# Hybrid SSD/MLA/GLA encoder on one core: the state-space heads' work taken up one head earlier, with other buffers and banks

## What is computed

```
proj = h @ w_in                                  # z, xbc, dt, q_a, kv_a
xbc  = silu(dwconv(xbc) + b);  xs, b_in, c_in = split(xbc)
dt   = softplus(dt_raw + dt_bias);  a = -exp(a_log)
# per head (16 of them), per direction (2), chunks of 128 tokens:
diff   = acum[l] - acum[s]
scores = (c @ b^T) * exp(where(causal, diff, -inf)) * dt[s]
y      = scores @ xs + (carried state) + xs * d_skip
y      = rmsnorm(y * silu(z))                    # two groups of 8 heads
o_mla  = attention(q_a, kv_a)                    # 8 latent attention heads
out    = concat(y, o_mla) @ w_out
```

## Time and profile before

| | us |
|---|---|
| median of 3 runs | 1443.49 (1442.85 to 1446.71) |
| the profiled execution | 1441.75 |
| its span, first to last instruction | 1439.6 |
| PE busy in it | 1379.3 (96%) |
| DVE busy | 822.8 (57%) |
| ACT busy | 646.5 (45%) |
| POOL busy | 639.9 (44%) |

### The profile page before, as it was taken

The page is one execution under the profiler, slowest core; times in us unless marked ns, Lnnn a source line. Parts: engine busy times, 40 slices in busy tenths (PEclk is TensorE's granted clock), DMA queues, the critical chain, the costliest instruction groups (busy, mean ns, idle before and its releaser), DMA issues.

```text
span 1439.6 us, 16672 instructions
## 1 busy us (share of the span) xinstructions
PE 1379.3 (96%) x6690; PEld 1138.9 (79%) x6690; DVE 822.8 (57%) x981; ACT 646.5 (45%) x985; POOL 639.9 (44%) x291
## 2 busy tenths in 40 slices
PE   6999988989999999999999999987999999999997
PEld 6778656767888888888888877875798888888886
DVE  5657597662027998887001654355168998884003
ACT  4544685554245544344323475434454544343221
POOL 2345495024533554545544243422714645445550
PEclk9999999999999999999999999998999999999998
DMA  5222100112322323323332312201213232323331
GB/s 188 86 92 88 37 1 19 33 45 88 99 77 90 101 93 98 95 95 94 93 95 86 114 59 88 88 30 44 73 45 131 89 102 89 102 85 94 96 92 59
DMA packets 36766, 117.89 MB, mean 82 GB/s; under 512 B 3857, under 2 KB 8337, under 8 KB 36689
## 3 DMA queue, kind: packets, MB, share of 16 engines
q1 hardware_dynamic: 35888, 114.63, 25.1%
q10 hardware_dynamic: 800, 2.20, 0.5%
HBM read 114.58 MB, written 2.10 MB: 81 GB/s over the span
## 4 chain that ended last, share of the span: by engine, by line
PE 76%; DVE 6%; ACT 3%; POOL 2%; issue 1%; DVEq 0%; ACTq 0%; POOLq 0%
PE bank L315 23%; PE bank L316 23%; PE bank L317 23%; PE bank L1169 1%; PE bank L1301 1%; POOL ebuf L987 1%; PE bank L1302 1%; POOL xdt L973 1%; PE bank L1777 1%; PE bank L1324 1%; DVE xres L562 1%; PE bank L405 1%; ACT prob L1373 1%; DVE m_ffn L555 0%; PE bank L1505 0%
## 5 line engine op out<-in xcount | busy, mean ns | idle before, releaser
L298 POOL TENSOR_TENSOR wlo<-raw,whi 128x1024 fp32r<-128x1024 f32 (+2 forms) x216 | 530.7, 2471 | 697.3 <-ACT whi L292 697.3
L315 PE MATMUL bank<-xw_hi,whi 128*128 128x512 f32 (+1 forms) x1360 | 516.6, 380 | 16.3 <-DVE xw_lo L581 11.7
L317 PE MATMUL bank<-xw_hi,wlo 128*128 128x512 f32 (+1 forms) x1360 | 505.8, 372 | 0.0
L316 PE MATMUL bank<-xw_lo,whi 128*128 128x512 f32 (+1 forms) x1360 | 505.8, 372 | 0.0
L292 ACT ACTIVATE whi<-raw 128x1024 fp32r<-128x1024 f32 (+2 forms) x217 | 220.6, 1023 | 216.5 <-DMA raw<-in_fout 111.8
L315 PEld LDWEIGHTS bank<-xw_hi,whi 128*128 128x128 f32 x1360 | 259.9, 191 | 67.8 <-issue 16.4
L316 PEld LDWEIGHTS bank<-xw_lo,whi 128*128 128x128 f32 x1360 | 259.8, 191 | 47.3 <-issue 3.6
L317 PEld LDWEIGHTS bank<-xw_hi,wlo 128*128 128x128 f32 x1360 | 259.5, 191 | 45.1
L534 DVE RECIPROCAL small<-small 128x2 f32<-128x2 f32 (+1 forms) x12 | 2.0, 170 | 352.7 <-ACT small L471 337.4
L638 DVE SCALAR_TENSOR_TENSOR cbuf<-ubuf,par,cbuf 128x510 f32<-128x510 f32 x100 | 170.8, 1708 | 3.5
L315 PE MATMUL bank<-g_hi,whi 128*128 128x512 f32 (+1 forms) x396 | 146.0, 369 | 0.1
(11 more groups left out here) (251 smaller groups left out, 1435.2 us busy)
## 6 DMA issues: line engine op xcount, KB each, us to landing
raw<-in_fin SPq DMA_DIRECT2D x88, 512.0 KB, 3.5
raw<-in_fout SPq DMA_DIRECT2D x32, 448.0 KB, 3.2
raw<-in_gin SPq DMA_DIRECT2D x25, 512.0 KB, 3.6
raw<-in_hin SPq DMA_DIRECT2D x24, 512.0 KB, 3.6
raw<-in_hout SPq DMA_DIRECT2D x16, 512.0 KB, 3.5
raw<-in_fout SPq DMA_DIRECT2D x16, 512.0 KB, 3.5
raw<-in_gout SPq DMA_DIRECT2D x8, 512.0 KB, 3.6
xres<-in_x SPq DMA_DIRECT2D x8, 256.0 KB, 7.5
```

The lines of the kernel that those rows point to most:

```text
L298: engine.tensor_tensor(wlo[s][:, 0:n], raw[s][:, 0:n], whi[s][:, 0:n].bitcast(F32), ALU.subtract).then_inc(w_lo, 1)
L315: first = nc.tensor.matmul(out_ap, wh, ah, start=start, stop=False)
L316: nc.tensor.matmul(out_ap, wh, al, start=False, stop=False)
L317: return first, nc.tensor.matmul(out_ap, wl, ah, start=False, stop=stop)
```

## The change

The diff moves work to earlier places and gives other buffers. It adds and removes no arithmetic.

- **Banks.** Block 20 goes to bank 0, blocks 21 and 23 to bank 7, block 22 to bank 6. The wait for `cb_set` moves from block 21 to block 22.
- **Buffers.** `ebuf3` lies in the region of the projection's input, `ebuf2` behind `xtok[0]` instead of over it, so the wait for xdt 0 to 3 is gone. Head 3's first step on ACT waits instead for the last block of the projection. The rotary key gets buffers of its own (`kr_part`).
- **Head 2 into the projection.** PE spreads head 2 after block 22, ACT takes its exponentials before silu of block 22, DVE its difference and mask before it scales block 23, POOL its mask after the weight part of block 25.
- **One head ahead.** DVE's turn n now holds the difference of head n+3 and the mask of head n+2. `gated` stays where it was. ACT's squares come one odd turn later.
- **POOL.** The 768 column weight part and both parts of xdt 4 stand ahead of mask 3. The additions of squares stand in even turns from 8 on.
- **End.** The sum of squares on PE stands after y(14) instead of y(13), and the two products of the rotary key ahead of gated(7).

The core of the diff:

```diff
-            return bank[(4, 5)[j] if j < 2 else 7 - j % 2 if j >= 20 else (0, 1, 3)[(j - 2) % 3]]
+            return bank[(4, 5)[j] if j < 2 else 6 + j % 2 if j >= 21 else (0, 1, 3)[(j - 2) % 3]]
...
             def gate(j):
                 his(act, base + j)
+                if j == 22:
+                    act_exps(act, 2)
...
             for n in range(HEADS):
-                if n + 2 < HEADS:
-                    dve_least(dve, n + 2)
-                if n >= 2:
-                    dve_mask(dve, n)
+                if n + 3 < HEADS:
+                    dve_least(dve, n + 3)
+                if 1 <= n < HEADS - 2:
+                    dve_mask(dve, n + 2)
                 if n % 2 and n >= 3:
                     gated((n - 3) // 2)
             dve_mla_low(dve)
+            dve_mla_rotated(dve)
             gated(KD - 1)
...
-            if n == 2:
-                act.wait_ge(sem("xdt_pool"), 4)
-                act.wait_ge(sem("xdt_dve"), 4)
+            if n == 3:
+                act.wait_ge(mm, BASE["hin"] + 24)
...
+            los(pool, BASE["mla"] - 1)
             pool.wait_ge(sem("xtok_dve"), NBLK)
-            for n in range(2, HEADS):
+            pool_xdt(pool, 4, 0)
+            pool_xdt(pool, 4, 1)
+            for n in range(3, HEADS):
                 pool_mask(pool, n)
-                if n < 10:
-                    pool_xdt(pool, 4 + (n - 2) // 2, n % 2)
-                if n % 2 and n >= 7:
-                    add_square((n - 7) // 2)
-                if n == HEADS // 2:
-                    los(pool, BASE["mla"] - 1)
+                if n < 9:
+                    pool_xdt(pool, 5 + (n - 3) // 2, (n - 3) % 2)
+                if n % 2 == 0 and n >= 8:
+                    add_square((n - 8) // 2)
```

More of the change, by code:

```diff
@@ L140, in build_program @@
             xdt = [None, None] + [sb(f"xdt{p}", 2 * NBLK * P, F32, s) for p in range(2, PAIRS * 2)]
+            ebuf3 = sb("ebuf3", 3 * T, F32, s)
+        with ExitStack() as s:
+            kr_part = [sb(f"kr_part{i}", T, F32, s) for i in range(2)]
         with ExitStack() as s:
@@ L160, in build_program @@
                 xbc = sb("xbc", 12 * T, F32, q)
-                with ExitStack() as q2:
-                    xtok = [sb("xtok0", NBLK * T, F32, q2), xtok_late]
-                ebuf_late = [sb(f"ebuf{i}", 3 * T, F32, q) for i in (2, 3)]
+                xtok = [sb("xtok0", NBLK * T, F32, q), xtok_late]
+                ebuf2 = sb("ebuf2", 3 * T, F32, q)
                 sqbuf = [sb(f"sqbuf{i}", T, F32, q) for i in range(2)]
@@ L183, in build_program @@
             sb("zbuf_mq", 12 * T, F32, s)
-            ebuf = [sb(f"ebuf{i}", 3 * T, F32, s) for i in range(2)] + ebuf_late
+            ebuf = [sb(f"ebuf{i}", 3 * T, F32, s) for i in range(2)] + [ebuf2, ebuf3]
             cbm = sb("cbm", 4 * 3 * SEQ, F32, s)
@@ L1102, in square @@
                                      ACT.Square).then_inc(sem("ssd_sq"), 1)
-            for n in range(2, HEADS):
+            for n in range(3, HEADS):
                 act_exps(act, n)
-                if n % 2 and n >= 5:
-                    square((n - 5) // 2)
+                if n % 2 and n >= 7:
+                    square((n - 7) // 2)
+            square(KD - 3)
             act_mla_prep(act)
@@ L1242, in pe_mla_prep, with dve_mla_rotated @@
             nc.tensor.matmul(bank[3][:], con("selrot"), ck(mq, 0), start=True, stop=True).then_inc(sem("mla_kr"), 1)
+        def dve_mla_rotated(dve):
+            dve.wait_ge(sem("rope_in"), 16)
+            dve.wait_ge(sem("mla_kr"), 1)
+            for i in range(2):
+                nc.vector.tensor_tensor(kr_part[i][:], bank[2 + i][:], cosin[:, i * T:(i + 1) * T],
+                                        ALU.mult).then_inc(sem("mla_kd"), 1)
         def dve_mla_prep(dve):
-            dve.wait_ge(sem("mla_kr"), 1)
-            nc.vector.tensor_tensor(ubuf[0][:], bank[2][:], cosin[:, 0:T], ALU.mult).then_inc(sem("mla_kd"), 1)
-            nc.vector.tensor_tensor(ubuf[1][:], bank[3][:], cosin[:, T:2 * T], ALU.mult).then_inc(sem("mla_kd"), 1)
             dve.wait_ge(sem("mla_kd"), 2)
```

25 lines of the change are left out of this document (13 added, 12 removed).

## The result

The changed kernel takes 1434.58 us (median of 4 runs, 1433.61 to 1435.58), the kernel before 1443.17 in the same comparison (4 runs, 1442.76 to 1446.71). The ratio is 0.9934 (0.992 to 0.9949), 8.6 us less.

A forecast was written before the change was run, and what follows sets the result against it. DVE and POOL, not PE, were taken to bound the SSD heads. The steps' -5.4 us at full clock plus 0.8 for the clock gave -4.6, set against the median of 1443.49: 1438.9 us, range 1435.0 to 1442.5.

The forecast's parts named there:

- Part 3: At y(4): a new wait of about 1.6 us for DVE's skip step, start at 183.3 against 186.05, -2.7.
- Part 1: Banks: block 21's wait for `cbm` goes, everything up to y(0) moves by -1.24 us, y(0) at 168.1.
- Part 2: Heads 1 to 3: PE's waits up to y(3) go; POOL's mask 3 runs 176.5 to 178.3, just in time.
- Part 4: Heads 4 to 8: a pair still takes 7.45 us, y(8) at 198.2, gain unchanged at -2.6.
- Part 5: y(9) and y(10): POOL no longer late, pair takes 6.8 us, y(10) at 205.0, -6.3, 3.7 of it here.
- Part 6: Heads 10 to 15: y(14) waits some 1.1 us for the skip step, 0.36 before; gain shrinks to -5.2 at y(15).
- Part 7: The end: two rotary key products go ahead of gated(7), -0.2 us, from bounds of -0.6 and +0.7.
- The clock: Behind the new wait at y(4): +0.8 us for a possible 1.2 GHz stretch, half of 0 to 1.7.
- new waits for the skip step go on through all heads: Rival: skip steps of pairs 0 to 5 each come 1 to 1.6 us late, about 1441 us; 18%.
- No new wait at all: Rival: DVE's masks fall between POOL's instructions, y(4) starts 1.6 us earlier, 1435.1 at full clock; 8%.
- a slower kernel by the clock: Rival: waits at y(4), y(6), y(8), y(14) leave PE at 1.2 GHz; six stretches cost 10.2 us, 1448.3; 6%.
- the lead isn't used: Rival: DVE and POOL share a port, total work is the same, only the banks' gain counts, about 1442 us; 5%.

The follow-up runs named there:

- e9: Changed kernel with POOL's masks narrowed from 768 to 256 columns from head 3 on, part of the masks left out: 1429.85 us (one run).
- e11: Kernel before with POOL's masks narrowed from 768 to 256 columns from head 3 on, part of the masks left out: 1435.32 us (one run).
- e8: Changed kernel with unused matmuls in PE's waits for the first softmax and in the last attention's normalisation: 1436.83 us (6 runs).
- e5: Changed kernel with the old banks and waits of blocks 21 to 23: 1437.4 us (7 runs), ratio 0.9961.
- e2: Kernel before with only the banks of blocks 20 to 23 and their waits changed: 1440.76 us (11 runs), ratio 0.9995.
- e6: Changed kernel with POOL's old order, weight part in turn 8 and xdt 4 behind masks 3 and 4: 1435.38 us (3 runs).
- e10: Changed kernel with DVE's old lead, difference of head n+2 and mask of head n in turn n: 1441.1 us (one run).
- e4: Changed kernel with three unused matmuls in PE's wait for the first softmax: 1436.1 us (5 runs), ratio 0.9965.
- e3: Changed kernel with DVE's skip step ahead of the mask of its turn: 1437.14 us (6 runs), ratio 0.9964.

## Why the prediction was right and wrong, step by step

**What bounds the kernel: shown.** DVE and POOL as a pair in the SSD heads. e9 and e11 take work from POOL and free PE and DVE. The rule of the Trainium skill that the prediction cited ("SBUF — State Buffer", section "Who interferes with whom"), that such instructions of the two engines exclude each other for their whole length, agrees with these runs: where POOL's addition takes 1.27, its time alone, DVE's mask beside it takes 2.04 and ends 0.8 behind it, and where DVE's mask takes 0.95, its time alone, POOL's addition takes 2.12 (changed kernel and e8). With mere sharing both would be longer. The sign that the prediction gave, y(4) at 181.7 or 183.3, does not decide: y(4) started at 182.54, for another reason (part 3).

**The sum of the steps: nearly right, in part by luck.** Forecast -5.4 at full clock, measured -4.8 (-5.9 in e8's trace, by the race). The product that I had near 232.3 stands at 232.61, its wait of 0.63 is gone. By parts:

- Part 1, -1.24 for the banks: measured -1.45 at y(0), and 1.5 at the scores by e5. The step's sentence that everything up to y(0) moves was right. It took for granted that the later parts keep it, which they did in the change, and did not in e2's trace.
- Part 2, mask 3 on POOL at 176.5 to 178.3, "just in time": it ran from 176.24 to 178.77, in 2.53 instead of 1.8, and PE waited 1.17. The start was right. The mask itself was priced as if alone, in a stage in which the prediction had just said that none is alone.
- Part 3, y(4) at 183.3 with 1.6 of new wait for the skip step: y(4) at 182.54, with no such wait. DVE's skip step was done at 181.25, not at 183. The step had added up to 1.4 to each of masks 4 and 5 for POOL, and they took 1.10 and 1.50 instead of 0.96: here it was POOL that stood back, with 2.53 for mask 3 and 2.55 for mask 4, and y(4) is late because y(3) waited for mask 3. The skip step's wait came at y(6), with 1.26, once DVE's masks 6 and 7 took 2.27 each. The wait was foreseen, its place and its cause at y(4) were wrong.
- Part 4, 7.45 a pair: from y(4) to y(8) 198.08 - 182.54 = 15.54, so 7.77 a pair. y(8) at 198.08 against 198.2: luck, since y(4) came 0.8 earlier than forecast and the two pairs took 0.6 longer.
- Part 5, y(10) at 205.0: 204.86. The 3.7 between y(8) and y(10) is what the trace shows too (-2.29 to -5.98). **The attribution was half of it.** I gave it to the weight part and the addition. With POOL's old order it is indeed 1.2 by y(10) and 0.1 by y(11) (e6: -4.36 to -5.60 and -4.47). But the weight part and xdt 4, placed early, cost 2.1 up to y(8) (-4.36 against -2.29), which part 2 had put at nothing, so that POOL's order nets 0.5 to 1.6. And without DVE's lead the term is gone as well: 1.0 by y(10) and nothing at y(11), there with a stretch at 1.2 GHz (e10: -3.29 to -4.32 and -2.82). The step didn't name the lead as a condition.
- Part 6, one wait of 1.1 before y(14): there were 0.79 at y(12) and 1.64 at y(14). The gain fell to -4.2 at y(15), where I had -5.2. This is the mis-sized term of the sum. Two DVE masks of 3.20 us together stand ahead of the skip step, where the step had counted on one. The step's own numbers don't give -5.2 either: 1.1 of wait less the 0.36 of before is 0.74, and -6.3 would shrink to -5.6. The wait at y(12) depends on who gets ahead of whom: in e8, where DVE's mask 13 goes first, it is missing and y(14) waits 1.17.
- Part 7, -0.2: -4.24 to -4.81, so -0.6, the better of its two bounds.

**The clock in the stage: no loss.** I added 0.8 for a stretch at 1.2 GHz behind the new waits. None of them, up to 1.64 us, was followed by one in the three traces of the changed kernel. The stretch that followed the old 1.75 us is gone, in the changed kernel 200 to 215 has a mean of 1.00:

```profile
200.00:215.00 15.00, 14.21 (x79) 9.37 (x79) 14.22 (x25) 12.81 (x26) 15.00 (x8) 1.00 0.00 1
```

**The miss of the range: the step "The clock".** This is the step that failed. It worked from the sum to a time as if the rest of the program took the same in every run: whatever lies outside the stage stood in the sum at nothing, and the range was drawn from the times of the rivals, without a term for it. In the first comparison the stage gave 4.8 of the 8.6, so 3.8 came from outside it. From the forecast of 1438.9 to the measured 1434.58 it is 4.3: these 3.8, 0.3 because the median of before was 1443.17 and not 1443.49, and 0.2 because the stage gave 4.8 where the sum had 4.6. In that last part two errors cancel, the +0.8 for a stretch at 1.2 GHz that never came and the 0.6 by which the -5.4 was too large.

Most of the 3.8 doesn't belong to the change: over all runs the gain is 6.1, and the same kernel, run again, shows where times come and go. Between its first trace and its last, 1433.61 and 1438.69, C times B already starts 2.85 later (148.23 and 151.08), with mean clocks of 0.89 from 0 to 30 us and 0.66 from 50 to 60 in the last and 1.00 in the first. 2.2 more come after the scores, for which the stretch 780 to 800 can account with up to 1.8 (an estimate: 20 us at a mean of 0.91 instead of 1.00, if PE is the bound there). The first comparison had four runs of the changed kernel, all from 1433.6 to 1435.6. All 17 runs have a mean of 1436.6, inside the range, as is the mean of the 13 later ones, 1437.2. So the miss is the draw of the first four runs together with a range too narrow for it. The prediction had what it needed to see this: its four times of the kernel before, 1441.75 to 1446.71, spread over 5.0 us.

**What stays open.** The means of all runs differ by 6.1, the stage by 4.8. Of the remaining 1.3, 0.14 lie outside the span (1.89 us there in the changed kernel, 2.03 before). In the changed kernel the mean clock is 0.9863 (17 runs), before 0.9854 (49 runs). A difference of 0.0009 over 1440 us is 1.3, which would fit. But the standard error of the 6.1 is 0.5, and the race at mask 13 moves the stage by 1.1 in an unknown share of the runs. So this is only argued: whether the change makes low-clock stretches elsewhere rarer, or the runs drew them so, was not settled. The runs e4 and e8 say only that a higher clock alone need not bring time. Open is also what decides the race, and how often it goes either way.

**The rivals.** That new waits for the skip step go on through all heads was half true: there are four, at y(6), y(8), y(12) and y(14), 4.3 us in all, but none at y(10), and the gain isn't used up. No new wait at all, and a slower kernel by the clock, did not occur. That the lead isn't used, and only part 1 counts, is refuted by the table: the gain goes to -5.98 by y(10), where part 1 alone gives -1.5, and without the lead (e10) less is left.

## What to carry to other kernels

Where two engines exclude each other, count their instructions one after the other, and price every one that is moved at what it takes beside the other engine; then reordering within the pair mostly moves the wait (e3, e6), while taking work from POOL shortened the stage by 5.7 to 6.1 us. Test an edit both ways, alone in the old kernel and left out of the whole, and follow it instruction by instruction: the bank edit kept its 1.5 us in one and lost it late in the other, to a race at a later head. Measure a change of a few microseconds between two fixed instructions around it: that repeated to 0.03 us in four traces here, when the whole kernel varied by 5. But take more than one trace, since the fifth was 1.1 off. And when a few runs of a kernel spread over 5 us, give the range of a forecast that much room, however exact the sum is.
